# A two-layer decoder trunk on one core: block-sum copies all queued behind slabs 8 to 17, and the first accumulating transfers moved from slabs 16 and 17 to behind slab 15's taps

## The reference

```python
def conv_sgu_mixer(x, ...):                      # layer 0
    h = x @ w_in                                 # 1024 -> 2048
    a = h[..., :512] * sigmoid(h[..., 512:1024])
    a = causal_depthwise_conv(a, conv_w, width=31) + conv_b
    a = silu(layer_norm(a))
    z = gelu(h[..., 1024:]);  u, v = split(z)
    v = layer_norm(v)
    sv = einsum('hts,bnshc->bnthc', w_spatial * causal, v) + b_spatial
    return concat([a, u * sv]) @ w_out           # 1024 -> 1024

def dilated_attention_mixer(x, positions, ...):  # layer 1
    ...                                          # 3 head groups, rotary, window softmax, merge

def swiglu(x, w_gate, w_up, w_down):             # 1024 -> 2816 -> 1024
    return (silu(x @ w_gate) * (x @ w_up)) @ w_down

for layer in range(2):
    x = layer_norm(alpha * x + mixer[layer](x))
    x = layer_norm(alpha * x + swiglu(x, ...))
```

## Time and profile before

| | |
|---|---|
| time, median of 3 runs | 1362.9 us (1362.55 to 1363.74) |
| profiled execution, its own time | 1363.81 us |
| its span in the profile | 1360.8 us |
| mean granted TensorE clock | 0.992 of full speed |
| PE busy | 1334.3 us (98%) |
| PE weight loads busy | 1188.9 us (87%) |
| DVE busy | 969.5 us (71%) |
| ACT busy | 664.0 us (49%) |
| POOL busy | 407.3 us (30%) |
| share of the ending chain | PE 88%, DVE 6%, the others 1% each or less |
| DMA | 203.49 MB, mean 150 GB/s |

### The profile page before, as it was taken

The page is one execution under the profiler, slowest core; times in us unless marked ns, Lnnn a source line. Parts: engine busy times, 40 slices in busy tenths (PEclk is TensorE's granted clock), DMA queues, the critical chain, the costliest instruction groups (busy, mean ns, idle before and its releaser), DMA issues.

```text
span 1360.8 us, 20871 instructions
## 1 busy us (share of the span) xinstructions
PE 1334.3 (98%) x8007; PEld 1188.9 (87%) x8007; DVE 969.5 (71%) x1299; ACT 664.0 (49%) x1027; POOL 407.3 (30%) x250
## 2 busy tenths in 40 slices
PE   8998999999979999999999999999999999999997
PEld 7886899999978889888888888888889999999885
DVE  3996698888868866777542677644238888889977
ACT  4465555555545654333432334333446455556566
POOL 5787610000011026455544544444243000000002
PEclk9999999999989999999999999999999999999999
DMA  9567623433499534887375777545122434335653
GB/s 285 195 215 164 139 79 96 121 92 106 123 269 280 182 93 137 212 192 187 94 204 148 178 188 174 131 131 157 54 63 70 117 92 112 104 93 201 202 167 135
DMA packets 208172, 203.49 MB, mean 150 GB/s; under 512 B 11397, under 2 KB 164761, under 8 KB 207800
## 3 DMA queue, kind: packets, MB, share of 16 engines
q1 hardware_dynamic: 188104, 173.37, 42.3%
q0 software_dynamic: 13376, 24.91, 10.3%
q10 hardware_dynamic: 6624, 4.29, 1.2%
HBM read 198.30 MB, written 54.05 MB: 185 GB/s over the span
## 4 chain that ended last, share of the span: by engine, by line
PE 88%; DVE 6%; DMA 1%; ACT 1%; issue 1%; POOL 1%; SPq 1%; DVEq 0%; ACTq 0%; POOLq 0%
PE pq L1199 9%; PE pq L1201 9%; PE pq L1202 9%; PE pq L874 8%; PE pq L876 8%; PE pq L875 8%; PE pq L896 7%; PE pq L897 7%; PE pq L898 7%; DVE pq L2064 3%; PE pq L1383 3%; PE pq L1385 3%; PE pq L1384 3%; PE pq L1362 1%; PE pq L1321 1%
## 5 line engine op out<-in xcount | busy, mean ns | idle before, releaser
L748 POOL TENSOR_TENSOR w_lo<-stage,w_hi 128x1024 fp32r<-128x1024 f32 x110 | 273.4, 2490 | 368.3 <-ACT w_hi L1456 368.2
L1456 ACT ACTIVATE w_hi<-stage 128x1024 fp32r<-128x1024 f32 (+1 forms) x186 | 192.3, 1049 | 177.0 <-PE pq L898 85.5
L874 PE MATMUL pq<-xt_hi,w_hi 128*128 128x512 f32 (+1 forms) x624 | 228.3, 366 | 0.5 <-DVE xt_lo L1965 0.4
L876 PE MATMUL pq<-xt_hi,w_lo 128*128 128x512 f32 (+1 forms) x624 | 225.2, 361 | 0.0
L875 PE MATMUL pq<-xt_lo,w_hi 128*128 128x512 f32 (+1 forms) x624 | 225.1, 361 | 0.0
L1199 PE MATMUL pq<-xt_hi,w_hi 128*128 128x256 f32 x632 | 179.5, 284 | 8.5 <-ACT u_kept L1693 8.5
L1201 PE MATMUL pq<-xt_lo,w_hi 128*128 128x256 f32 x632 | 179.4, 284 | 0.0
L1202 PE MATMUL pq<-xt_hi,w_lo 128*128 128x256 f32 x632 | 179.4, 284 | 0.0
L874 PEld LDWEIGHTS pq<-xt_hi,w_hi 128*128 128x128 f32 x624 | 117.9, 189 | 19.5 <-DVE xt_lo L1965 1.2
L1199 PE MATMUL pq<-xs_hi,w_hi 128*128 128x256 f32 x472 | 134.0, 284 | 0.0
L1201 PE MATMUL pq<-xs_lo,w_hi 128*128 128x256 f32 x472 | 133.9, 284 | 0.0
(11 more groups left out here) (283 smaller groups left out, 2969.4 us busy)
## 6 DMA issues: line engine op xcount, KB each, us to landing
stage<-in_od_w_qkv_dram SPq DMA_DIRECT2D x72, 512.0 KB, 4.1
stage<-t_rows SPq DMA_DIRECT2D x46, 512.0 KB, 3.6
stage<-in_ffn_w_gate_dram SPq DMA_DIRECT2D x44, 512.0 KB, 4.9
stage<-in_ffn_w_up_dram SPq DMA_DIRECT2D x44, 512.0 KB, 4.0
t_rows<-in_ffn_w_down_dram SPq DMA_DIRECT2D x38, 512.0 KB, 7.0
stage<-in_ffn_w_down_dram SPq DMA_DIRECT2D x25, 512.0 KB, 4.1
t_rows<-in_ffn_w_down_dram POOLq DMA_DIRECT2D x19, 512.0 KB, 7.8
t_rows<-in_ffn_w_down_dram POOLq DMA_DIRECT2D x38, 256.0 KB, 6.4
```

Source lines behind the costliest of these rows:

```text
L748: pool.tensor_tensor(w_lo[slab % RING][:, :], w_stage[slab % RING][:, :], w_hi[slab % RING][:, :].bitcast(F32), ALU.subtract).then_inc(w_l ...
L874: pe.matmul(o, hi[:, k, :], x_hi, start=(k == 0), stop=False)
L876: last = pe.matmul(o, lo[:, k, :], x_hi, start=False, stop=(k == KD - 1))
L1456: act.activation(w_hi[slab % RING][:, 0:width], w_stage[slab % RING][:, 0:width], ACT.Copy).then_inc(w_hi_ready, 1)
```

## The change

Four edits. `COPY_BEHIND` gets eight entries instead of six, so that the copies of all eight pairs are issued behind the slabs 8, 9, 10, 11, 12, 14, 15 and 17; the loop that issued pairs 6 and 7 behind the gate and up loads goes. The sixteen early accumulating transfers, before two behind the split of each of the slabs 16 to 23 and ahead of its taps, are now three behind slab 15's taps, none in slabs 16 and 17, and then 2, 2, 3, 2, 2, 2 behind slabs 18 to 23. The later sixteen: those from the third on (before from the fourth on) wait for ACT's copy of a slab of the down projection, and each for the slab one later than before.

```diff
-COPY_BEHIND = (8, 10, 12, 15, 17, 19)
-SUMS_FROM = 16
+COPY_BEHIND = (8, 9, 10, 11, 12, 14, 15, 17)
+SUMS_BEHIND = {15: 3, 18: 2, 19: 2, 20: 3, 21: 2, 22: 2, 23: 2}
@@ sync
             load_up(S_UP0, 0)
-            for j in range(len(COPY_BEHIND), PAIRS[0]):
-                copy_blocks(0, j)
             for q in range(TILES):
                 sp.dma_start(pos_i[q * ROT:(q + 1) * ROT], ...)
@@ gpsimd
+            sums_begun = 0
             for slab in range(S_UP0):
                 split_low(slab)
-                for step, j in EARLY_SUMS[2 * max(slab - SUMS_FROM, 0):2 * max(slab - SUMS_FROM + 1, 0)]:
-                    block_sum(0, step, j)
                 if slab == 17:
...
                         pool.tensor_tensor(acc[:, c, :], acc[:, c, :], tap_sum[:, c, :], ALU.add
                                            ).then_inc(chunk_summed, 1)
+                for _ in range(SUMS_BEHIND.get(slab, 0)):
+                    block_sum(0, *EARLY_SUMS[sums_begun])
+                    sums_begun += 1
             norm(0, S_UP0)
...
             for n, (step, j) in enumerate(LATER_SUMS):
-                if n >= 3:
-                    pool.wait_ge(w_hi_ready, plain(S_DOWN0 + n - 3) + 1)
+                if n >= 2:
+                    pool.wait_ge(w_hi_ready, plain(S_DOWN0 + n - 2) + 1)
                 block_sum(0, step, j)
```

## The result

The changed kernel takes 1347.55 us (median of 4 runs, 1346.26 to 1348.16), the kernel before 1362.72 (4 runs beside it, 1362.30 to 1363.74): ratio 0.9886, 95% interval 0.9869 to 0.9903, 15.2 us faster. The profiled execution took 1347.21 us, with a span of 1345.2. In the experiments two executions, 2213.54 us of e1 and 3420.11 us of e4b, are slow from start to end and left out of every median here.

What follows compares the result with a forecast made beforehand. PE, busy 98% of the span, was taken as the bound, so only its waits and half clock could be won. Median 1362.9 less 3.8 (front) and 10.8 (back) gave 1348.3 us, range 1345.8 to 1353.0.

Steps and rivals of the forecast that it cites:

- rival B: Front: DVE is not held at line 2154, so the front gains 5.3 us; 1346.8 us, chance 0.24.
- Removed from POOL's chain: Front: transfers leaving slabs 16 and 17 take 3.91 us off POOL's chain, so line 834 ends at 108.47.
- The hold at line 2154: Front: POOL's split of slab 20 starts first and holds DVE's addition till 119.8; front gain 3.8 us.
- The stricter reading: Front: line 2152 keeps POOL out until 117.45, then either may have the port; if VectorE, gain 5.3 us.
- Copies forward: Slabs before 16: pairs riding earlier, seven sets instead of four, make no slab late; 0, bound 0.5 us.
- The first down slab: Back: without copies in front it lands 5.1 us after issue, ending u_kept's wait and half clock; gain 10.8 us.
- The latest harmless landing: Back: the first down slab may land until 378.7 before PE waits for u_kept.
- Rival C: Back: first down slab still lands late, at 382.3, behind THREEs and norm loads; 1352 to 1354 us, chance 0.13.
- the price of a set: Slab loads: one set of copies stretches the load behind it by 3.4 us.
- The later sums: Down projection: sums start one slab, 2.7 us, later; PE does not wait; 0, bound 0 to 2.7, gain excluded.
- Rival E: Down projection: FOURs come too late for slab 18, making the kernel slower; about 1384 us, chance 0.04.
- Rival D: Front: the clock falls all the same, costing half of 3.42 us, 1.7 more; 1350.0 us, chance 0.08.

Runs made afterwards that it cites:

- e1: Kernel before with only POOL's early sums moved (three behind slab 15, none behind 16 and 17), copies and later sums unmoved: 1357.95 us, ratio 0.9970.
- e4b: Changed kernel with three small writes ahead of DVE's last addition of the squares (line 2154), to start it behind POOL's split: median 1348.6 us.
- e2: Kernel before with only the copies moved (eight sets behind slabs 8 to 17), early and later sums unmoved: 1351.87 us, ratio 0.9924.
- e3: Changed kernel with one of the eight sets of copies put back in front of the first down slab: 1346.88 us, ratio 0.9889.
- two behind slab 16: Changed kernel with the first four early sums spread as two behind slab 15 and two behind slab 16: 1348.59 us, ratio 0.9903.

## Why the prediction was right, and where it was not

The time, 1347.55, lies between the forecast's 1348.3 and rival B's 1346.8.

*Removed from POOL's chain.* 3.91 us forecast, 3.95 found (112.38 to 108.43). The cover held: three issues of 3.1 us went into 3.23 us of idle time. No wait at line 1015, as forecast.

*The hold at line 2154: the step that failed.* The forecast had the addition at 117.5 and the split at 117.25, so a hold till 119.8, a wait of 1.5 us, and 3.8 us of gain. The addition was right to 0.02; the split came at 117.54, 0.29 later than worked out, because ACT's copy that releases it moved by 5.5 us (121.92 to 116.40) and not by 5.8. DVE was first, POOL was held for 0.5 us instead, which nothing waited for, and the front gained 5.0. That is rival B, in mechanism and size (5.3). With the order turned round, the forecast's wait comes as it was described and so does its time, 1348.46. It is 1.14 us where 1.5 were worked out, and that was in the sum: by the earlier trace rows a split of 2.37 us from 117.25 ends at 119.62 and line 2154 0.55 behind it, at 120.17, a wait of 1.1. The rule of the hold was right; what failed was the order of the two starts, given 2 to 1 where my steps could not tell them apart. That the time lies in the forecast's own range (1347.3 to 1349.5) is luck: B ran, and the times of the two orders are only 0.9 apart. The stricter reading, with line 2152 keeping POOL out, was not tried: ACT released the split at 117.46, line 2152 ended at 117.48, and the split began 0.08 behind ACT, as in the kernel before.

That DVE is first is not chance: in the seven profiles in which nothing was put in front of it (the changed kernel, e1, e2, e3, two behind slab 16, both with the down projection's sums moved) DVE is 0.02 to 0.05 us ahead each time, since both hang on PE's work. In the forecast this order was open; the profiles fix it.

*Copies forward.* 0 forecast and found: no wait of PE for a slab in 30 to 106 us. The forecast's list of pairs is wrong (all but pair 0 ride earlier, 2 and 4 too), but its count, seven sets instead of four until slab 16, is right, and only that was used.

*The first down slab.* Forecast: issued near 366.6, landing 5.1 us. Found: 364.92 and 3.1, shorter than the lower bound of 3.6. The gain of the back was 10.8 forecast, 10.6 found, because beyond the spare an early slab wins nothing. The latest harmless landing, 378.7 in the old time and so 373.6 with 5.1 us won in front of it, agrees with e3: 372.7 less 0.7 of wait, plus the 1.6 us by which e3 is early, is 373.6. Rival C did not come; the price of a set, 3.4, was 4 to 5.5.

*The later sums.* 0 forecast, bound 0 to 2.7 lost, a gain excluded. Taken with the other edits there is no loss, but the reason against a gain was wrong: that PE had no wait there in the kernel before says nothing of a kernel in which PE arrives 10 us sooner. The edit saves 1.7 us of what the other one would cost. The FOURs took 8.1 to 11.9 us, not 7.3 to 8.7, and slab 18 landed 1.2 us before ACT took it, not 3.3. There is more behind that: DVE splits it only at 431.92. Rival E was as far off as thought.

*The clock.* Rival D did not come, and a single wait of 1.73 us did not bring it either.

Open: why the kernel before got half its clock at 113.09 and e2 did not, behind the same two waits (1.7 and 2.0 us). It makes 1.2 us of the front's gain uncertain. The kernel before differs from itself as well: of its 12 executions beside e1 three have a mean granted clock of 0.995 and took 1359.64 to 1361.47 us, the other nine 0.992 or 0.993 and 1361.06 to 1364.26. So it need not be the copies moved in e2 that made the difference; the means do not tell which stretch it was.

## What to carry to other kernels

When a wait goes, read the stage behind it again for the new arrival times: what shared the DMA engines or a port harmlessly before may now stand in the way, and the edit that costs nothing alone may be what makes the other one pay. Work put into an engine's idle time ahead of a wait is free up to that idle time, and the same work one step later cost here nearly its full length (1.8 of 1.9 us). Where two starts on engines that hold each other out fall within a few tenths of a microsecond, give both orders near equal chances, and if the order matters, fix it in the code.

## What the runs showed of the hardware

A slab load of 128x1024 took 3.1 us with no set of copies in front of it, 7.0 behind one set of three and 11.9 and 12.5 behind two. The same eight accumulating transfers landed after 7.4 to 9.8 us when they were issued from 392.1 on, after 8.1 to 11.9 from 398.7 on, and after 5.6 to 11.8 from 403.8 on, where the last four took 7.2 to 5.6. Half clock came behind two waits of 1.7 and 2.0 us in one execution and not in another, not with a single one of 1.73, and it came with one of 3.0. An addition of DVE with both inputs in SBUF, begun 0.35 us behind a split of POOL, ended 0.55 us after it; begun 0.02 us ahead, it took its 0.69, and the split took 2.90 us instead of 2.41.
